# Products that nothing reads, placed in front of seven of TensorE's waits

## The reference

```python
# layer 0: multi-scale causal pooling mixer, then SwiGLU
h = einsum(window means of x minus x, pool_w) * pool_scale
x = layer_norm(ALPHA * x + h); x = layer_norm(ALPHA * x + swiglu(x))
# between the layers: shared latent and queries' latent
kv = x @ wkv_a                  # 1024 -> 256 + 64, RMS norm of 256, rotary of 64
q  = rms_norm(x @ wq_a) @ wq_b  # 1024 -> 384 -> 8 heads of 128 + 64
# layer 1: latent attention (8 heads), wo, layer norm, SwiGLU, layer norm
```

## Time and profile before

| what | value |
|---|---|
| device time, 3 runs | median 2543.57 us (2538.87 to 2545.26) |
| profiled execution, device time | 2539.54 us |
| its span, first to last instruction | 2537.5 us |
| TensorE matmul busy | 2392.3 us, 94% of the span |
| VectorE, ScalarE, GpSimd busy | 51%, 30%, 13% |
| mean granted clock of TensorE | 0.979 |

### The profile page before, as it was taken

How to read it: one execution, slowest core, us unless ns; L and a number is a source line. 1 busy time by engine, 2 the same in 40 slices (tenths; PEclk the granted TensorE clock), 3 DMA queues, 4 the chain that set the end, 5 groups by cost and what they waited for, 6 DMA issues and landing times.

```text
span 2537.5 us, 35304 instructions
## 1 busy us (share of the span) xinstructions
PE 2392.3 (94%) x14022; PEld 2178.8 (86%) x14022; DVE 1287.9 (51%) x2435; ACT 768.2 (30%) x1469; POOL 330.6 (13%) x300
## 2 busy tenths in 40 slices
PE   7899999999999968999998889799999999999997
PEld 7799999999999868898987677587998989999996
DVE  4733343333334675677767787635243443333336
ACT  2331111111111333555546566413311111111112
POOL 2400000000000410000006545033000000000006
PEclk9999999999999989999999999799999999999998
DMA  4121111111111031000005444321211110111111
GB/s 162 42 67 34 50 50 30 36 50 50 50 50 63 13 114 43 19 19 1 12 22 157 155 156 156 133 79 34 67 44 41 50 44 25 50 50 50 51 42 67
DMA packets 137073, 153.84 MB, mean 61 GB/s; under 512 B 10256, under 2 KB 114224, under 8 KB 136808
## 3 DMA queue, kind: packets, MB, share of 16 engines
q1 hardware_dynamic: 124656, 110.07, 13.9%
q0 software_dynamic: 12288, 41.95, 5.3%
HBM read 142.24 MB, written 10.32 MB: 60 GB/s over the span
## 4 chain that ended last, share of the span: by engine, by line
PE 82%; DVE 10%; ACT 3%; issue 3%; DMA 1%; POOL 0%; SPq 0%; ACTq 0%; DVEq 0%
PE ps L216 23%; PE ps L218 23%; PE ps L217 23%; DVE split L209 4%; PE ps L2136 2%; PE ps L2101 2%; ACT split L204 2%; PE ps L2116 1%; PE ps L2117 1%; PE ps L224 1%; PE ps L223 1%; PE ps L1646 1%; PE ps L2123 1%; DVE plain L292 1%; DVE plain L1889 1%
## 5 line engine op out<-in xcount | busy, mean ns | idle before, releaser
L216 PE MATMUL ps<-split 128*128 128x512 f32 (+6 forms) x3632 | 1236.8, 341 | 56.9 <-DVE split L209 31.9
L217 PE MATMUL ps<-split 128*128 128x512 f32 (+6 forms) x3632 | 1222.8, 337 | 0.0
L218 PE MATMUL ps<-split 128*128 128x512 f32 (+6 forms) x3632 | 1222.3, 337 | 0.0
L216 PEld LDWEIGHTS ps<-split 128*128 128x128 f32 x3632 | 689.6, 190 | 102.6 <-DVE split L209 37.0
L217 PEld LDWEIGHTS ps<-split 128*128 128x128 f32 x3632 | 689.8, 190 | 38.3 <-issue 1.5
L218 PEld LDWEIGHTS ps<-split 128*128 128x128 f32 x3632 | 689.9, 190 | 37.3
L204 ACT ACTIVATE split<-plain 128x1024 fp32r<-128x1024 f32 (+8 forms) x446 | 313.6, 738 | 594.8 <-PE ps L224 365.5
L209 DVE TENSOR_TENSOR split<-plain,split 128x1024 fp32r<-128x1024 f32 (+7 forms) x422 | 362.9, 884 | 190.3 <-ACT split L204 187.1
L998 DVE TENSOR_TENSOR plain<-plain,ps 128x350 f32<-128x350 f32 (+1 forms) x132 | 68.0, 515 | 552.9 <-ACT plain L952 552.3
L276 DVE TENSOR_TENSOR plain<-plain,ps 128x512 f32<-128x512 f32 x360 | 245.0, 685 | 197.0 <-PE ps L218 192.2
L209 DVE TENSOR_TENSOR split<-ps,split 128x512 fp32r<-128x512 f32 (+5 forms) x480 | 247.1, 554 | 136.6 <-ACT split L204 134.6
(11 more groups left out here) (147 smaller groups left out, 1432.1 us busy)
## 6 DMA issues: line engine op xcount, KB each, us to landing
plain<-w_gate SPq DMA_DIRECT2D x44, 512.0 KB, 4.6
plain<-w_up SPq DMA_DIRECT2D x44, 512.0 KB, 4.0
plain<-w_down SPq DMA_DIRECT2D x44, 512.0 KB, 4.4
plain<-x_prompt SPq DMA_DIRECT2D x8, 512.0 KB, 11.2
x_spill<-plain SPq DMA_DIRECT2D x1, 4096.0 KB, 13.9
plain<-wo SPq DMA_DIRECT2D x8, 512.0 KB, 5.3
plain<-x_spill SPq DMA_DIRECT2D x8, 512.0 KB, 7.2
y_prompt<-plain SPq DMA_DIRECT2D x8, 512.0 KB
```

The costliest lines, as they stand in the source:

```text
L216: pe.matmul(out, still[0], moving[0], start=start, stop=False)
L217: pe.matmul(out, still[0], moving[1], start=False, stop=False)
L218: return pe.matmul(out, still[1], moving[0], start=False, stop=stop)
```

## The change

Seven runs of products are put in front of waits of TensorE. Their results are written to PSUM banks that are free at that time, and nothing reads them: 12 in front of the first wait of the program (they read ones, which VectorE writes with a memset as its first instruction), 40 in the first seam, 16 and 22 in steps 9 and 10 of the FFN's last stage, 52 in front of latent unit 9, and 9 each in the last two steps of the latents. No other instruction moves against its neighbours.

```diff
+def keep_busy(pe, k, times, bank, rows, width):
+    for _ in range(times):
+        pe.matmul(k.ps[:, bank, 0:width], rows[:, 0:P], rows[:, 0:width], start=True, stop=True)
...
     def between(step):
+        if layer == 0 and step == FIRST_PRODUCTS[1]:
+            keep_busy(pe, k, 40, 7, k.xt_hi[:, 0, :], 350)
         if step in FIRST_PRODUCTS:
...
 def mixer_pe(pe, k):
     s, nt = k.s, k.ns + k.nm
+    pe.wait_ge(s["warm"], 1)
+    keep_busy(pe, k, 12, UNIT_BANKS[1], k.xt_hi[:, 0, :], BANK)
     pe.wait_ge(s["kept_in"], 16)
...
     def latent_products(self, pe):
         def between(step):
+            if step == self.k.tiles + 1:
+                keep_busy(pe, self.k, 16, 3, self.k.wd[:, 0, 0, :], BANK)
+            if step == self.k.tiles + 2:
+                keep_busy(pe, self.k, 22, 3, self.k.wd[:, 0, 0, :], BANK)
             if step >= self.k.tiles + 2:
...
     for step in range(2, latent_tasks(k) + 3):
+        if step == half:
+            pe.wait_ge(s["lat_w_lo"], 5)
+            keep_busy(pe, k, 52, 7, k.lat_w(4)[0][:, 0, :], k.q_w)
+        if step > latent_tasks(k):
+            keep_busy(pe, k, 9, 7, k.lat_w(4)[0][:, 0, :], k.q_w)
         if step < latent_tasks(k):
...
         def _(dve):
+            dve.memset(k.xt_hi[:, 0, 0:BANK].bitcast(F32), 1.0).then_inc(k.s["warm"], 1)
             page_index_dve(dve, k)
```

## The result

The changed kernel took a median of 2529.8 us in seven runs (2527.3 to 2534.4), the kernel before 2543.57 us in seven runs on the same chip. The ratio is 0.9949, with a 95% interval of 0.9938 to 0.9961: 13.0 us faster (9.9 to 15.8). The two profiled executions differ by 10.2 us (2539.54 and 2529.34 us; spans 2537.5 and 2527.3).

What follows compares the result with a forecast made beforehand. It took TensorE, busy 94% of the span, as the bound, with the prize in slow-clock work after waits. Terms 0 + 1.6 + 0 + 2.3 + 0.6 = 4.5 us gave 2539 against the median; forecast 2538.5, range 2531 to 2544.

Steps and rivals of the forecast that it cites:

- the sum: Whole kernel: the gains at start, seam, latents, unit 9 and heads add up to 4.5 us.
- Start, 0 with 5.0 as the other end: First work: about 4.4 us idle behind 12 products loses the clock, gain 0; 5.0 us if it holds.
- First seam, 1.6: Seam's second group: clock holds over 2.0 us idle, 13 matmuls take 2.1 us not 3.7, 1.6 us gained.
- In front of the latents, 0: Latent unit 0: 1.3 us saved, but ScalarE's wait for the key row's store hides it, so 0.
- In front of unit 9, 2.3: Latent unit 9: 16 matmuls take 2.8 us not 5.1; all 2.3 us get through.
- Heads, 0.6 of 1.3: Heads: 1.3 us if the clock holds over 2.86 us without products, nothing if it falls; half taken, 0.6.
- The two cases: Heads: clock holds through the wait for GpSimd's weights, 1.3 us gained, or falls, nothing gained.
- From the profile to the median: Whole kernel: profiled 2539.54 us was 4.0 below the median 2543.57; the clock's timing can be part of that.
- The start's rival: Start: clock is up at 10.94 us and stays, 5.0 us more, 9.5 gained, about 2533.5; chance 0.13.
- the slower one: Added products run at 1.2 GHz; unit 9 starts 4.0 us late, 2547.6 us; chance 0.06.
- The rest gains nothing: Within the slower rival: apart from unit 9's 4.0 us delay, nothing is gained, giving 2547.6 us.

Runs made afterwards that it cites:

- the shift alone: Kernel before plus 64 semaphore increments on TensorE at the start, no added products: 2537.9 us, ratio 0.9974.
- the middle alone: Changed kernel without the products of start and heads and without the memset, 50 instead of 52 in front of unit 9: 2538.4 us, ratio 0.9981.
- the kernel before's second profile: Kernel before, unedited, profiled once more: one execution of 2546.1 us, span 2544.0.
- the shift of 128: Kernel before plus 64 narrow products at the start, 128 instructions more: 2534.0 us, ratio 0.9959.
- the late one: Kernel before plus 32 narrow products just ahead of the second layer's FFN, 64 instructions more: 2537.2 us, ratio 0.9969.
- The narrow products in its place: Changed kernel with the 52 products in front of unit 9 cut to 16 columns and 32 weight columns each: 2534.05 us, ratio 0.9955.
- the longer runs: Changed kernel with start, seam and heads runs extended to the end of their waits and 7 products before the third group: 2525.2 us, ratio 0.9927.

## Why the prediction was wrong

**The step that failed is the sum.** "0 + 1.6 + 0 + 2.3 + 0.6 = 4.5 us" counts the seven waits and takes everything else as not moved. The 320 added instructions move all later code of TensorE, and by that the jumps back of the second FFN's loop, 3.4 to 3.7 us in its queue before where they were slow, take 0.2 us. The missing term is 6.6 us (4.1 to 9.2) as the shift alone measures it, 4.5 us by the medians of those runs, and 5.2 us between the two profiled executions, since one of the three jumps was fast in the kernel before's. It was to be seen: the row `PE ps L216 <- issue: 9.8, 5, 5.5` has five waits where only one belongs to the latents, and the prediction looked at TensorE's waits from 131 to 850 only. With that term the prediction's own sum gives 2538.5 - 6.6 = 2531.9 us, for 2529.8 measured. The sum of the seven waits itself held: 4.8 us for the middle alone, where 3.9 were forecast, and 3.8 in the trace for 4.5. But the seam's term came out right in part by luck, as told below.

The Trainium skill (Runtime: NRT & Kernel Launch, Instruction fetch mechanics) says that instructions come in blocks of 256, TensorE's store holding 2048, that the fetch runs ahead in sequence, and that "A taken branch whose target isn't in the current 2-page window forces a DMA fetch of the target page before execution can continue". The traces agree with a stall at a taken branch and with a period of 256. They do not agree with a window of two blocks for TensorE: loops of 1624 instructions jump back in 0.2 us at eleven places modulo 256, and one packet of instructions moved in the changed kernel's 400 us. A loop that stays in the store of 2048 unless the fetch has run on past its end would fit, but no run here shows what is in the store, so why just these places are bad stays open.

**Start, 0 with 5.0 as the other end: right, and for the reason given.** 4.04 us without a matmul (4.4 forecast), clock 0.50 from 10.9 us on, pairs of 0.72 us. Without the gap it gives 4.7 us in the trace and 5.7 in the times, the 5.0 of the other end.

**First seam, 1.6: 1.7 in the trace, in part by luck.** The clock was 1.00 behind the wait, but not over 2.0 us of idle time, as forecast: the clock had fallen in the mixer's tail, so TensorE came to the wait at 103.17 and not 99.3, and the 40 products ended at 109.82, just behind VectorE's split. The trace therefore doesn't test the 2.0 us, nor whether a gain would have been there without that fall. The fall in the mixer's tail is not the change's: the kernel before's second profile has it too, at 82.4. The third group, which was to stay slow, was slow for 3.4 us and not 6.8; kernels without a product in the seam (the shift of 128, the late one) have 3.4 us there too, so this is not shown to be the change's.

**In front of the latents, 0: right.** Unit 0 gained its 1.3 us, and ScalarE's wait for the store took it back, growing from 5.03 us to 6.76. In all that wait took back 1.7 us: x_spill, issued 1.02 us earlier, landed after 14.2 us and not 13.9, so of what the seam and the end of the FFN had gained only a part got past it. Another 0.6 us went at 925.7, where the clock fell for 3.4 us and had not in the kernel before.

**In front of unit 9, 2.3: 2.3.** 16 matmuls in 2.80 us at 1.00, released by VectorE, all of it still there at 976. The narrow products in its place lose 1.9 us there in the trace.

**Heads, 0.6 of 1.3: 0.1.** The clock fell at 997.4, 0.9 us after the first product, behind 3.01 us of idle time. The two cases were 0 and 1.3, and the 0.6 was neither. With 13 more products in that wait the clock held, and the heads gave 1.6 us more.

**From the profile to the median.** The prediction noted that its profiled execution was 4.0 us below the median and named the clock's timing as what could be a part of that. A part was the third jump: 1.9 to 2.6 us by the third passes of 139.6 and 140.4 us in the two other profiles with the loop at that place. The clock had its part too: the second profile reaches the first jump 4.9 us later than the first, and two dips that the first does not have, at 82.4 in the mixer's tail and at 1024.5, make 1.2 and 1.5 of them.

**The rivals.** The start's rival (0.13, 2533.5) did not come about; the 52 added products took 9.29 us, 0.18 each, so the slower one did not either. "The rest gains nothing" had been counted in none of them.

## What to carry to other kernels

An edit that only adds instructions also moves code, and a hardware loop can be several microseconds slower or faster for where its branch comes to lie: look for waits with no releaser ("issue") at a jump back and for branch instructions of over 1 us, and time both kernels with a shift of 64 instructions too before a small difference is put down to the edit. Filler products have to reach to the end of the wait, or nearly so. Here the clock was up for the next unit with 1.03 and 1.39 us left, and in the longer runs with 0.33, 0.42 and 0.55; 4.04 and 3.01 us left gave nothing and 0.1 us; with 0 left the start gave its whole 4.7 us. It is no fixed limit: in the seam of the kernel before the clock outlasted 5.3 us without a matmul. And what they gain ends at the next wait that has another cause, here a store behind a 4 MB transfer.

## What was not expected of the hardware

A jump back over 1624 instructions takes TensorE's queue 0.21 to 0.24 us, or 3.4 to 3.8 us at a bad place of the loop, which comes again after 256 instructions, and 1.6 to 2.7 us of that reach the array. In the kernel before one of three jumps at the same place was fast, so it is also a matter of timing. A semaphore increment on TensorE takes 0.151 us: 64 end at 10.63 us. The granted clock of 1.00 that the profile of the kernel before prints from 11 to 22 us is no measurement: pairs go at 0.72 us there, and at 0.42 us when the clock was up before them.
